# Four-way and eight-way interleaved moving operands in the out- and down-projection of a hybrid attention layer

## The chip, the cores and the metric

The kernel runs on one core of one Trainium2 chip. The metric is the device time of one execution in microseconds (us), as the median of a few runs. TensorE does the matmuls and its weight loads, VectorE (DVE), ScalarE (ACT) and GpSimd (POOL) do the elementwise work, and SyncE (SP) issues the transfers.

## The reference, cut to what matters

The layer works on 256 tokens of width 2048, all in float32:

```
h     = RMSNorm(x);  proj = h @ w_in            # 2048 x (6 * 1024 + 8)
o_f   = forgetting attention, 8 heads of 128    # group A
o_d   = differential attention, 8 heads of 128  # group B
x     = x + concat(o_f, o_d) @ w_out            # out-projection, 2048 x 2048
u     = RMSNorm(x) @ w_up                       # up-projection, 2048 x 11008
u     = causal conv of width 3 along the tokens
out   = x + (silu(gate) * val) @ w_down         # down-projection, 5504 x 2048
```

## The kernel before, in words

The reference is float32, and the matmuls are in a faster float32 form (`F32R`) that keeps fewer bits. So each operand is split into a rounded part (hi) and the rest (lo). ACT writes hi as a rounding copy (`split_hi`, line 534, for weights), DVE writes lo as the difference (`split_lo`, line 816). A product is the sum of hi x hi, hi x lo and lo x hi.

All weights stream in pieces of 128 x 1024 (128 x 768 for the input projection) through a ring of four slots: SP loads `raw`, ACT makes `w_hi`, DVE makes `w_lo`, and PE uses the piece and frees it (`piece_used`). PE works through the stages in this order: the input projection for one head after another, with the attention of the previous head laid between its pieces by hand; the out-projection (32 pieces, 256 weight blocks of 128 x 128); the up-projection (172 pieces); the down-projection (86 pieces, 688 weight blocks).

In the last three stages the weights are the stationary operand and the activations move. One weight block takes two matmuls (`mm3_features`, lines 277 to 281). The first (line 279) has the hi weights and moves 512 columns: hi and lo of one activation tile of 256 tokens. The second (line 280) has the lo weights and moves the 256 hi columns. The first writes a whole PSUM bank of 512 columns, the second adds into the upper half of that bank. So hi x hi stands in the lower half and the two mixed products in the upper half, and the result is the sum of both halves.

The columns do not move in the order in which they lie in SBUF. `weave` reads the tile alternately from two places that are 256 elements (1024 bytes) apart: element 0, element 256, element 1, element 257, and so on. `part` gives the layout of a tile that goes with it: with two ways a tile is [hi of tokens 0-127, lo of tokens 0-127, hi of 128-255, lo of 128-255], so that alternating reads give first all hi columns and then all lo columns, with tokens 0, 128, 1, 129, ... in this order. PSUM therefore holds the tokens of the out- and down-projection in alternating order, and `by_parity` reads them back with a step of two elements where the sum is taken (lines 1113 and 1115 for the out-projection, 1214 and 1220 for the down-projection); `by_half` walks the natural order in SBUF beside it. `mixed` holds the activation tiles of the out-projection (written at lines 592 and 934), `a_s` those of the down-projection (lines 771 and 1170), `xs` those of the up-projection (lines 737 and 1120), which are laid out so that PSUM comes out in natural order.

In the down-projection eight output tiles are summed at once, one for each bank: all 43 pieces of the first eight tiles, then all 43 of the second eight. The first piece of the second eight has to wait tile by tile until DVE has read the bank (`o_done`).

Before any weights land, PE runs 19 matmuls on a tile of ones, `warm_r`, in four shapes; the weights of each are columns 0 to 127 of the same tile:

```
for _ in range(WARM_UP + 2):                     # 10, line 375: 512 columns as they lie
...
for rhs in (weave(warm_r[:]), warm_r[:].rearrange("p (a b) -> p b a", a=4), weave(warm_r[:, 0:S])):
    for _ in range(3):                           # line 378: three of each
```

Of the kernel before, what the change touches and what calls it, by code (L numbers as in the profile page):

```python
# [9 lines left out]
ALU = mybir.AluOpType  # L10
ACT = mybir.ActivationFunctionType
AX_X = mybir.AxisListType.X

P = 128
S, D, F = 256, 2048, 5504
# [4 lines left out]
KT = D // P  # L20
# [7 lines left out]
RING = 4  # L28
# [9 lines left out]
DOWN0 = UP0 + UP_PIECES  # L38
ALL_PIECES = DOWN0 + DOWN_PIECES
OCTET = 8  # L40
SROW = P + S


# [19 lines left out]
def hybrid_layer_kernel(nc, xT_d, xtok_d, w0_d, win_d, wrest_d, const_d, row_d, vec_d, out_d):  # L63
    c_d = nc.dram_tensor("c_scratch", (H, S), F32, kind="Internal").ap()
    with ExitStack() as ctx:
# [8 lines left out]
        w_hi = sb("w_hi", RING * PW, F32R)  # L74
        w_lo = sb("w_lo", RING * PW, F32R)
        xT = sb("xT", KT * S)
# [12 lines left out]
        a_t = sb("a_t", S)  # L89
        xu = sb("xu", 2 * S)  # L90
        ms2 = y2_t[:, S:2 * S]

        with ExitStack() as att:
            def sa(name, cols, dt=F32, parts=P):
                return sb(name, cols, dt, parts, att)
            mixed = sa("mixed", KT * 2 * S, F32R)
# [37 lines left out]
        a_s = sb("a_s", FT * 2 * S, F32R)  # L134
# [25 lines left out]
        mixhi_done, mixlo_done = sem("mixhi_done"), sem("mixlo_done")  # L160
# [4 lines left out]
        xu_done, x1_done, x1hi_done, x1sq_done = sem("xu_done"), sem("x1_done"), sem("x1hi_done"), sem("x1sq_done")  # L165
# [3 lines left out]
        a_done, a_hi, a_lo = sem("a_done"), sem("a_hi"), sem("a_lo")  # L169
# [4 lines left out]
        def bank(b, lo=0, n=512):  # L174
            return ps[:, b * 512 + lo:b * 512 + lo + n]

        def f32(ap):
            return ap.bitcast(F32)

        def slot(t, s, n=PW, at=0):  # L180
            return t[:, s * PW + at:s * PW + at + n]

        def tile(t, i, n=S, width=S, at=0):

            return t[:, bass.ds(i * width + at, n)]

        def weave(ap):

            return ap.rearrange("p (k q) -> p q k", k=2)

        def part(t, h):

            return t.rearrange("p (k h j) -> p h k j", k=2, h=2)[:, h]

        def by_half(ap):
            return ap.rearrange("p (k j) -> p k j", k=2)

        def by_parity(ap):
            return ap.rearrange("p (j k) -> p k j", k=2)

        ident = const[:, C_ID:C_ID + P]
        block = ctx.enter_context(nc.Block())
# [61 lines left out]
        def _(pe):  # L264
# [9 lines left out]
                    last = pe.matmul(o, xl, wh, start=False, stop=(kt == KT - 1), skip_group_check=True)  # L274
                return last

            def mm3_features(b, s, t, acts, start, stop):

                pe.matmul(bank(b), slot(w_hi, s, P, t * P), weave(acts), start=start, stop=False, skip_group_check=True)  # L279
                return pe.matmul(bank(b, S, S), slot(w_lo, s, P, t * P), part(acts, 0).rearrange("p k j -> p j k"),  # L280
                                 start=False, stop=stop, skip_group_check=True)

            def transposes(f, p, kind):
# [92 lines left out]
            for rhs in (weave(warm_r[:]), warm_r[:].rearrange("p (a b) -> p b a", a=4), weave(warm_r[:, 0:S])):  # L376
                for _ in range(3):
                    pe.matmul(scratch[:, 0:rhs.shape[1] * rhs.shape[2]], warm_r[:, 0:P], rhs, start=True, stop=True,
                              skip_group_check=True)

            for g, (h, b) in enumerate(PAIR):
                pe.wait_ge(split_done, g + 1)
                for k2 in range(2):
                    if h == 0:
                        pe.wait_ge(xs_ready, 2 * b + k2 + 1)
                    last = mm3_tokens(h, QKV if h else QKV + H, 2 * b + k2, g % RING, k2)
# [42 lines left out]
            for b in range(8):  # L429
                pe.wait_ge(split_done, OUT0 + b + 1)  # L430

                for t in (0, 1, 4, 5, 2, 6, 3, 7) if b == 0 else range(8):
                    kt, n = 2 * b + t // 4, t % 4
                    if b == 0 and t == 0:
                        pe.wait_ge(evac_done, 4 * (HEADS - 1))
                    if b == 0 and t in (2, 3):
                        pe.wait_ge(evac_done, 4 * HEADS - 3 + t)
                    if kt >= KT - 2 and n == 0:
                        pe.wait_ge(mixlo_done, kt + 1)
                    mxt = mixed[:, kt * 2 * S:(kt + 1) * 2 * S]  # L440
                    last = mm3_features(n, b % RING, t, mxt, kt == 0, kt == KT - 1)
                last.then_inc(piece_used, 1)
                attention_steps(HEADS, 1, "fox", b, OUT_AT)

            def out_pair(i, first):

                for b in range(4):
                    pe.wait_ge(split_done, i * 4 + (OUT0 + 8 + b + 1))
                    if b % 2 == 0 and not first:
                        pe.wait_ge(x1_done, i * 2 + (3 + b // 2))  # L450
                    for t in range(8):
                        kt = 8 * (b % 2) + t
                        mxt = mixed[:, kt * 2 * S:(kt + 1) * 2 * S]
                        last = mm3_features(4 + b // 2, b, t, mxt, kt == 0, kt == KT - 1)
                    last.then_inc(piece_used, 1)

            out_pair(0, True)
# [26 lines left out]
            def down_piece(d, kt, s, edge=None):  # L484

                pe.wait_ge(split_done, d + (DOWN0 + 1))
                if edge == "start0":
                    pe.wait_ge(a_lo, FT - 2)
                    pe.wait_ge(r2_ready, 1)
                for n in range(OCTET):  # L490
                    if edge == "start0" and n == 6:
                        pe.wait_ge(g_sum, FT)
                        pe.wait_ge(v_sum, FT)
                    if edge == "start1":
                        pe.wait_ge(o_done, n + 1)
                    last = mm3_features(n, s, n, tile(a_s, kt, 2 * S, 2 * S),
                                        edge in ("start0", "start1"), False)
                last.then_inc(piece_used, 1)

            def last_two(d, s):  # L500

                pe.wait_ge(split_done, DOWN0 + d + 2)
                for n in range(OCTET):
                    for k in range(2):
                        kt = FT - 2 + k
                        a = a_s[:, kt * 2 * S:(kt + 1) * 2 * S]
                        last = mm3_features(n, s + k, n, a, False, k == 1)
                    if n < OCTET - 1:
                        last.then_inc(tile_summed, 1)
                last.then_inc(piece_used, 2)  # L510
# [17 lines left out]
        def _(act):  # L528
# [59 lines left out]
            def mix_hi(f, kind):  # L588

                act.wait_ge(pv_done if kind == "fox" else onorm_done, f)  # L590
                src = bank(B_O, 0, S) if kind == "fox" else on[:]
                act.activation(part(tile(mixed, f - 1, 2 * S, 2 * S), 0), by_half(src), ACT.Copy).then_inc(mixhi_done, 1)

            def square_o(f):
                act.wait_ge(pv_done, f)
# [59 lines left out]
            for b in range(4):  # L655
                if b == 2:
                    act.wait_ge(piece_used, PAIR_END0)
                    for m in range(M):
                        last = act.activation(z[:, m * H:(m + 1) * H], bank(m, QKV, H), ACT.Copy)
# [108 lines left out]
            def act_hi(i):  # L768

                act.wait_ge(a_done, i + 1)  # L770
                act.activation(part(tile(a_s, i, 2 * S, 2 * S), 0), by_half(a_t[:]), ACT.Copy).then_inc(a_hi, 1)

            def up_frame(i, first):
                for b in range(4):
# [38 lines left out]
        def _(dve):  # L813
# [116 lines left out]
            def mix_lo(f, kind):  # L930
                dve.wait_ge(mixhi_done, f)
                src = bank(B_O, 0, S) if kind == "fox" else on[:]
                mxt = tile(mixed, f - 1, 2 * S, 2 * S)
                dve.tensor_tensor(part(mxt, 1), by_half(src), part(f32(mxt), 0), ALU.subtract).then_inc(mixlo_done, 1)

            def forget_bias(f):

# [171 lines left out]

            def x1_tile(n, b, par):  # L1110

                u = by_half(xu[:, par * S:(par + 1) * S])
                dve.tensor_tensor(u, by_parity(bank(b, S, S)), by_half(tile(xT, n)), ALU.add).then_inc(xu_done, 1)
                dve.wait_ge(xu_done, n + 1)
                dve.tensor_tensor(by_half(tile(xT, n)), by_parity(bank(b, 0, S)), u, ALU.add).then_inc(x1_done, 1)  # L1115

            def x1_lo(n):
                dve.wait_ge(x1hi_done, n + 1)
# [48 lines left out]
            def act_lo(i):  # L1167
                dve.wait_ge(a_hi, i + 1)
                ast = tile(a_s, i, 2 * S, 2 * S)
                dve.tensor_tensor(part(ast, 1), by_half(a_t[:]), part(f32(ast), 0), ALU.subtract).then_inc(a_lo, 1)  # L1170

            def up_frame(i, first):

# [30 lines left out]
            def out_octet(o):  # L1204

                partial = [xu[:, 0:S], xu[:, S:2 * S], a_t[:], silu_t[:]]

                def add_second(n):
                    t = OCTET * o + n
                    if n < OCTET - 1:  # L1210
                        dve.wait_ge(tile_summed, (OCTET - 1) * o + n + 1)
                    else:
                        dve.wait_ge(piece_used, DOWN0 + FT * (o + 1))
                    dve.tensor_tensor(by_half(partial[n % 4]), by_parity(bank(n, S, S)), by_half(xT[:, t * S:(t + 1) * S]),
                                      ALU.add).then_inc(ou_done, 1)

                def add_first(n):
                    t = OCTET * o + n
                    dve.wait_ge(ou_done, t + 1)
                    dve.tensor_tensor(by_half(xT[:, t * S:(t + 1) * S]), by_parity(bank(n, 0, S)), by_half(partial[n % 4]),  # L1220
                                      ALU.add).then_inc(o_done, 1)

                add_second(0)
                for n in range(1, OCTET):
                    add_second(n)
                    add_first(n - 1)
                add_first(OCTET - 1)
# [138 lines left out]
```

## Time and profile before

| | |
|---|---|
| median of 3 runs | 1083.84 us (1083.58 to 1085.18) |
| the profiled execution | 1086.33 us |
| its span, first to last instruction | 1084.6 us |
| PE busy | 1063.9 us, 98% of the span |
| PE weight loads busy | 988.6 us, 91% |
| DVE / ACT / POOL busy | 774.7 / 626.1 / 132.0 us |
| read from HBM | 208.81 MB |

A matmul's busy time runs from its start to the modelled end of its drain, so successive matmuls overlap; the pace of PE is read from the starts of successive matmuls, not from the duration of one. PEclk is the clock granted to TensorE, as a share of full speed.

### The profile page before, as it was taken

To read this page: it belongs to the slowest core of one execution; us is meant where nothing else is said; L and a number is where in the kernel's file an instruction comes from. 1 tells how busy PE (TensorE), PEld (TensorE's weight loads), DVE (VectorE), ACT (ScalarE), POOL (GpSimd) and SP (SyncE) were. 2 spreads that over 40 slices of the span, in tenths; PEclk is the share of its full clock that TensorE was granted. 3 is DMA by queue.
4 is the path that set the end of the run, shared out by engine and by line. 5 is a ranking of instruction groups with operands and counts; after the bars stand their busy time and mean duration, and the time that the engine had idled before them with its cause. 6 is when DMAs were issued, how large, how long until landed. Compare 5 with 4: busy or idle time off the path is not lost.

```text
span 1084.6 us, 20254 instructions
## 1 busy us (share of the span) xinstructions
PE 1063.9 (98%) x6487; PEld 988.6 (91%) x6487; DVE 774.7 (71%) x1274; ACT 626.1 (58%) x1009; POOL 132.0 (12%) x170
## 2 busy tenths in 40 slices
PE   9889999999999999999999999999999999999998
PEld 8878988999998999999999999999999999999997
DVE  6677787776676877887887788787787744464444
ACT  6756665756565656666666666666666534334432
POOL 0222243000000212211111111111111100000000
PEclk9999999999999999999999999999999999999999
DMA  9654545465655765666666666666665666656664
GB/s 312 245 151 159 166 148 172 147 198 152 204 193 172 230 205 184 208 206 196 200 202 200 199 197 205 197 207 196 195 210 195 201 205 196 202 181 215 201 204 138
DMA packets 66762, 211.28 MB, mean 195 GB/s; under 512 B 9384, under 2 KB 11568, under 8 KB 66352
## 3 DMA queue, kind: packets, MB, share of 16 engines
q1 hardware_dynamic: 66736, 210.94, 61.1%
q8 instruction: 15, 0.25, 0.1%
q14 instruction: 11, 0.09, 0.0%
HBM read 208.81 MB, written 2.11 MB: 194 GB/s over the span
## 4 chain that ended last, share of the span: by engine, by line
PE 84%; DVE 7%; ACT 3%; POOL 2%; DMA 2%; issue 1%; SPq 0%; DVEq 0%; ACTq 0%; POOLq 0%
PE ps L279 45%; PE ps L280 23%; PE ps L272 4%; PE ps L274 4%; PE ps L273 4%; DVE w_lo L816 2%; DMA raw<-in_w 1%; ACT w_hi L534 1%; POOL qn L1251 1%; ACT s_sb L580 1%; DMA raw<-in_win 1%; DVE s_sb L884 1%; PE ps L289 1%; PE ps L298 1%; PE ps L318 0%
## 5 line engine op out<-in xcount | busy, mean ns | idle before, releaser
L816 DVE TENSOR_TENSOR w_lo<-raw,w_hi 128x1024 fp32r<-128x1024 f32 (+2 forms) x418 | 497.8, 1198 | 235.1 <-ACT w_hi L534 234.0
L534 ACT ACTIVATE w_hi<-raw 128x1024 fp32r<-128x1024 f32 (+2 forms) x418 | 414.0, 994 | 335.9 <-PE ps L280 272.0
L279 PE MATMUL ps<-xs,w_hi 128*128 128x512 f32 x1376 | 451.0, 382 | 0.0
L280 PE MATMUL ps<-xs,w_lo 128*128 128x256 f32 x1376 | 375.1, 273 | 0.0
L279 PEld LDWEIGHTS ps<-xs,w_hi 128*128 128x128 f32 x1376 | 260.1, 189 | 36.2
L280 PEld LDWEIGHTS ps<-xs,w_lo 128*128 128x128 f32 x1376 | 264.2, 192 | 0.0
L279 PE MATMUL ps<-a_s,w_hi 128*128 (+1 forms) x688 | 225.6, 382 | 0.1
L280 PE MATMUL ps<-a_s,w_lo 128*128 (+1 forms) x688 | 187.5, 273 | 0.0
L272 PE MATMUL ps<-w_hi,xs 128*128 128x384 f32 (+1 forms) x512 | 175.0, 342 | 2.3 <-DVE cT L1018 1.2
L273 PE MATMUL ps<-w_lo,xs 128*128 128x384 f32 (+1 forms) x512 | 167.6, 327 | 0.0
L274 PE MATMUL ps<-w_hi,xs 128*128 128x384 f32 (+1 forms) x512 | 167.6, 327 | 0.0
L279 PEld LDWEIGHTS ps<-a_s,w_hi 128*128 128x128 f32 x688 | 130.0, 189 | 18.6 <-DVE xT L1220 0.4
L280 PEld LDWEIGHTS ps<-a_s,w_lo 128*128 128x128 f32 x688 | 132.1, 192 | 0.0
L1296 POOL TENSOR_TENSOR u_t<-s_t,r2bc 128x256 f32<-128x256 f32 x86 | 71.6, 832 | 378.5 <-DVE s_t L1148 378.5
L272 PEld LDWEIGHTS ps<-w_hi,xs 128*128 128x128 f32 x512 | 97.4, 190 | 5.8 <-issue 2.3
L273 PEld LDWEIGHTS ps<-w_lo,xs 128*128 128x128 f32 x512 | 97.5, 190 | 0.3
L274 PEld LDWEIGHTS ps<-w_hi,xs 128*128 128x128 f32 x512 | 97.2, 190 | 0.0
L279 PE MATMUL ps<-mixed,w_hi 128*128 128x512 f32 x256 | 84.9, 384 | 0.5 <-DVE xT L1115 0.4
L280 PE MATMUL ps<-mixed,w_lo 128*128 128x256 f32 x256 | 69.8, 273 | 0.0
L757 ACT ACTIVATE y_t<-u_t,vec 128x256 f32<-128x256 f32 x86 | 51.5, 599 | 11.3 <-issue 6.1
L279 PEld LDWEIGHTS ps<-mixed,w_hi 128*128 128x128 f32 x256 | 48.4, 189 | 7.7 <-DVE xT L1115 0.7
L766 ACT ACTIVATE lo_t<-ps 128x256 f32<-128x256 f32 x86 | 32.5, 378 | 32.1 <-PE ps L280 32.1
(141 smaller groups left out, 705.3 us busy)
## 6 DMA issues: line engine op xcount, KB each, us to landing
raw<-in_wrest SPq DMA_DIRECT2D x290, 512.0 KB, 4.2
raw<-in_win SPq DMA_DIRECT2D x120, 384.0 KB, 3.7
raw<-in_w SPq DMA_DIRECT2D x8, 392.0 KB, 5.5
xT<-in_xT SPq DMA_DIRECT2D x8, 256.0 KB, 5.7
xtok<-in_xtok SPq DMA_DIRECT2D x2, 1024.0 KB, 8.2
out<-xT SPq DMA_DIRECT2D x16, 128.0 KB, 2.2
cbc<-c_scratch SPq DMA_DIRECT2D x1, 1024.0 KB, 6.8
const<-in_const SPq DMA_DIRECT2D x1, 512.0 KB, 9.3
```

The source lines that it names most:

```text
L272: pe.matmul(o, xh, wh, start=(kt == 0), stop=False, skip_group_check=True)
L273: pe.matmul(o, xh, wl, start=False, stop=False, skip_group_check=True)
L274: last = pe.matmul(o, xl, wh, start=False, stop=(kt == KT - 1), skip_group_check=True)
L279: pe.matmul(bank(b), slot(w_hi, s, P, t * P), weave(acts), start=start, stop=False, skip_group_check=True)
L280: return pe.matmul(bank(b, S, S), slot(w_lo, s, P, t * P), part(acts, 0).rearrange("p k j -> p j k"), start=False, stop=stop, skip_group_c ...
L289: last = pe.transpose(bank(B_T, i * P, P), qn[:, c:c + HD], ident)
L298: last = pe.matmul(bank(B_S + c, P, S), qkT[rows, P:S], qkT[rows, S:2 * S], start=True, stop=True, skip_group_check=True)
L534: act.activation(slot(w_hi, s, w), slot(raw, s, w), ACT.Copy).then_inc(hi_ready, 1)
L757: act.activation(y2_t[:, y2:y2 + S], u_t[:, u + 2:u + 2 + S], ACT.Identity, scale=tile(vec, i, 1, 8, V_CW + off + 2), bias=tile(vec, i, 1, ...
L766: act.activation(lo_t[:, lo:lo + S], bank(6 + (not gate), S, S), ACT.Copy).then_inc(g_lo if gate else v_lo, 1)
L816: dve.tensor_tensor(slot(w_lo, s, w), slot(raw, s, w), f32(slot(w_hi, s, w)), ALU.subtract).then_inc(split_done, 1)
L1296: pool.tensor_tensor(u_t[:, u:u + S], s_t[:, off:off + S], r2bc[:], ALU.mult).then_inc(g_u if gate else v_u, 1)
```

## The change: more places to read from

The four layout helpers get a parameter for the number of ways, 2 by default. The out-projection uses 4, the down-projection 8. With 4 ways a tile of 512 elements is four stretches of [64 hi, 64 lo], and the moving operand is read from four places 128 elements (512 bytes) apart in turn; with 8 ways it is eight stretches of [32 hi, 32 lo], read from eight places 64 elements (256 bytes) apart. The writers of `mixed` and `a_s` use the same layouts, and the sums are read from PSUM with a step of 4 or 8 elements. The input projection, the up-projection, the warm-up matmuls, the number and size of all instructions, the waits and the transfers stay as they are.

```diff
+OUT_WAYS, DOWN_WAYS = 4, 8
...
-        def weave(ap):
-            return ap.rearrange("p (k q) -> p q k", k=2)
-        def part(t, h):
-            return t.rearrange("p (k h j) -> p h k j", k=2, h=2)[:, h]
+        def weave(ap, k=2):
+            return ap.rearrange("p (k q) -> p q k", k=k)
+        def part(t, h, k=2):
+            return t.rearrange("p (k h j) -> p h k j", k=k, h=2)[:, h]
...
-            def mm3_features(b, s, t, acts, start, stop):
-                pe.matmul(bank(b), slot(w_hi, s, P, t * P), weave(acts), start=start, stop=False, skip_group_check=True)
-                return pe.matmul(bank(b, S, S), slot(w_lo, s, P, t * P), part(acts, 0).rearrange("p k j -> p j k"),
+            def mm3_features(b, s, t, acts, start, stop, k=2):
+                pe.matmul(bank(b), slot(w_hi, s, P, t * P), weave(acts, k), start=start, stop=False, skip_group_check=True)
+                return pe.matmul(bank(b, S, S), slot(w_lo, s, P, t * P), part(acts, 0, k).rearrange("p k j -> p j k"),
                                  start=False, stop=stop, skip_group_check=True)
...
-                u = by_half(xu[:, par * S:(par + 1) * S])
-                dve.tensor_tensor(u, by_parity(bank(b, S, S)), by_half(tile(xT, n)), ALU.add).then_inc(xu_done, 1)
+                u = by_half(xu[:, par * S:(par + 1) * S], OUT_WAYS)
+                dve.tensor_tensor(u, by_parity(bank(b, S, S), OUT_WAYS), by_half(tile(xT, n), OUT_WAYS), ALU.add).then_inc(xu_done, 1)
...
-                    dve.tensor_tensor(by_half(xT[:, t * S:(t + 1) * S]), by_parity(bank(n, 0, S)), by_half(partial[n % 4]),
+                    dve.tensor_tensor(by_half(xT[:, t * S:(t + 1) * S], DOWN_WAYS), by_parity(bank(n, 0, S), DOWN_WAYS),
+                                      by_half(partial[n % 4], DOWN_WAYS),
                                       ALU.add).then_inc(o_done, 1)
```

## Rows read from the trace of the kernel before

**Rows 1.** The page: busy time by engine, granted clock.

```profile
PE 1063.9 (98%) x6487; PEld 988.6 (91%) x6487; DVE 774.7 (71%) x1274; ACT 626.1 (58%) x1009; POOL 132.0 (12%) x170
...
PEclk9999999999999999999999999999999999999999
```

**Rows 2.** Stages out (two rows), up, down (two): busy us of each engine, PEclk, DMA.

```profile
318.63:351.54 32.91, 32.47 (x199) 29.66 (x200) 22.51 (x45) 17.67 (x29) 2.67 (x4) 1.00 0.50 160
351.54:403.90 52.36, 52.36 (x319) 48.23 (x320) 42.04 (x53) 31.65 (x43) 10.14 (x11) 1.00 0.69 217
403.90:855.20 451.30, 451.30 (x2757) 415.02 (x2757) 360.46 (x518) 285.22 (x431) 71.58 (x86) 1.00 0.63 200
855.20:970.15 114.95, 114.88 (x703) 105.23 (x701) 59.61 (x65) 48.01 (x48) 0.73 (x1) 1.00 0.61 197
970.15:1081.10 110.95, 110.95 (x676) 101.86 (x676) 54.55 (x55) 41.34 (x39) 0.00 (x0) 1.00 0.58 189
```

**Rows 3.** The page, costliest groups: the matmuls of the two changed stages, with counts.

```profile
L279 PE MATMUL ps<-a_s,w_hi 128*128 (+1 forms) x688 | 225.6, 382 | 0.1
L280 PE MATMUL ps<-a_s,w_lo 128*128 (+1 forms) x688 | 187.5, 273 | 0.0
...
L279 PE MATMUL ps<-mixed,w_hi 128*128 128x512 f32 x256 | 84.9, 384 | 0.5 <-DVE xT L1115 0.4
L280 PE MATMUL ps<-mixed,w_lo 128*128 128x256 f32 x256 | 69.8, 273 | 0.0
```

**Rows 4.** Timeline of PE in the down-projection: start us, us, engine, line, operation.

```profile
999.73 0.38 PE L279 MATMUL ps<-a_s,w_hi 128*128 x1
999.95 0.27 PE L280 MATMUL ps<-a_s,w_lo 128*128 x1
...
1002.68 0.38 PE L279 MATMUL ps<-a_s,w_hi 128*128 x1
```

**Rows 5.** Timeline of PE, warm-up: three 2-way, three 4-way, then 2-way of 256.

```profile
5.90 0.63 PE L378 MATMUL ps<-warm_r 128*128 128x512 f32 x1
6.32 0.63 PE L378 MATMUL ps<-warm_r 128*128 128x512 f32 x1
6.74 0.45 PE L378 MATMUL ps<-warm_r 128*128 128x512 f32 x1
7.03 0.44 PE L378 MATMUL ps<-warm_r 128*128 128x512 f32 x1
7.31 0.45 PE L378 MATMUL ps<-warm_r 128*128 128x512 f32 x1
7.59 0.45 PE L378 MATMUL ps<-warm_r 128*128 128x512 f32 x1
7.87 0.39 PE L378 MATMUL ps<-warm_r 128*128 128x256 f32 x2
7.98 0.39 PE L378 MATMUL ps<-warm_r 128*128 128x256 f32 x2
```

**Rows 6.** Timeline of the weight loads (PEld) in the same stretch.

```profile
6.75 0.26 PEld L378 LDWEIGHTS ps<-warm_r 128*128 128x128 f32 x1
7.03 0.19 PEld L378 LDWEIGHTS ps<-warm_r 128*128 128x128 f32 x1
```

**Rows 7.** Timeline of PE, input projection, 2-way reads of 384 columns (11 starts apart).

```profile
12.27 0.33 PE L272 MATMUL ps<-w_hi,xs 128*128 128x384 f32 x1
...
14.06 0.33 PE L274 MATMUL ps<-w_hi,xs 128*128 128x384 f32 x1
```

**Rows 8.** Groups by line and shape: DVE adds that read PSUM unstrided, with step two.

```profile
L1148 DVE TENSOR_TENSOR s_t<-ps,lo_t 128x256 f32<-128x256 f32 x86 | 35.9, 418 | 0.0
...
L1115 DVE TENSOR_TENSOR xT<-ps,xu 128x256 f32 x12 | 5.1, 424 | 0.4
```

**Rows 9.** Chain of waits where the second octet starts: start us, us, what.

```profile
965.12 0.67 DVE xu L1214 x2
...
970.15 0.48 PE ps L279
```

More of the change, by code:

```diff
@@ L185, in tile, with by_half, by_parity @@
             return t[:, bass.ds(i * width + at, n)]
-        def weave(ap):
-            return ap.rearrange("p (k q) -> p q k", k=2)
-        def part(t, h):
-            return t.rearrange("p (k h j) -> p h k j", k=2, h=2)[:, h]
[L195 to L199, printed above, removed]
+        def weave(ap, k=2):
+            return ap.rearrange("p (k q) -> p q k", k=k)
+        def part(t, h, k=2):
+            return t.rearrange("p (k h j) -> p h k j", k=k, h=2)[:, h]
+        def by_half(ap, k=2):
+            return ap.rearrange("p (k j) -> p k j", k=k)
+        def by_parity(ap, k=2):
+            return ap.rearrange("p (j k) -> p k j", k=k)
         ident = const[:, C_ID:C_ID + P]
@@ L440, in _ @@
                     mxt = mixed[:, kt * 2 * S:(kt + 1) * 2 * S]
-                    last = mm3_features(n, b % RING, t, mxt, kt == 0, kt == KT - 1)
+                    last = mm3_features(n, b % RING, t, mxt, kt == 0, kt == KT - 1, OUT_WAYS)
                 last.then_inc(piece_used, 1)
@@ L453, in out_pair @@
                         mxt = mixed[:, kt * 2 * S:(kt + 1) * 2 * S]
-                        last = mm3_features(4 + b // 2, b, t, mxt, kt == 0, kt == KT - 1)
+                        last = mm3_features(4 + b // 2, b, t, mxt, kt == 0, kt == KT - 1, OUT_WAYS)
                     last.then_inc(piece_used, 1)
@@ L496, in down_piece @@
                     last = mm3_features(n, s, n, tile(a_s, kt, 2 * S, 2 * S),
-                                        edge in ("start0", "start1"), False)
+                                        edge in ("start0", "start1"), False, DOWN_WAYS)
                 last.then_inc(piece_used, 1)
@@ L506, in last_two @@
                         a = a_s[:, kt * 2 * S:(kt + 1) * 2 * S]
-                        last = mm3_features(n, s + k, n, a, False, k == 1)
+                        last = mm3_features(n, s + k, n, a, False, k == 1, DOWN_WAYS)
                     if n < OCTET - 1:
@@ L591, in mix_hi @@
                 src = bank(B_O, 0, S) if kind == "fox" else on[:]
-                act.activation(part(tile(mixed, f - 1, 2 * S, 2 * S), 0), by_half(src), ACT.Copy).then_inc(mixhi_done, 1)
+                act.activation(part(tile(mixed, f - 1, 2 * S, 2 * S), 0, OUT_WAYS), by_half(src, OUT_WAYS), ACT.Copy).then_inc(mixhi_done, 1)
             def square_o(f):
@@ L770, in act_hi @@
                 act.wait_ge(a_done, i + 1)
-                act.activation(part(tile(a_s, i, 2 * S, 2 * S), 0), by_half(a_t[:]), ACT.Copy).then_inc(a_hi, 1)
+                act.activation(part(tile(a_s, i, 2 * S, 2 * S), 0, DOWN_WAYS), by_half(a_t[:], DOWN_WAYS), ACT.Copy).then_inc(a_hi, 1)
             def up_frame(i, first):
@@ L933, in mix_lo @@
                 mxt = tile(mixed, f - 1, 2 * S, 2 * S)
-                dve.tensor_tensor(part(mxt, 1), by_half(src), part(f32(mxt), 0), ALU.subtract).then_inc(mixlo_done, 1)
+                dve.tensor_tensor(part(mxt, 1, OUT_WAYS), by_half(src, OUT_WAYS), part(f32(mxt), 0, OUT_WAYS), ALU.subtract).then_inc(mixlo_done, 1)
             def forget_bias(f):
@@ L1110, in x1_tile @@
             def x1_tile(n, b, par):
-                u = by_half(xu[:, par * S:(par + 1) * S])
-                dve.tensor_tensor(u, by_parity(bank(b, S, S)), by_half(tile(xT, n)), ALU.add).then_inc(xu_done, 1)
+                u = by_half(xu[:, par * S:(par + 1) * S], OUT_WAYS)
+                dve.tensor_tensor(u, by_parity(bank(b, S, S), OUT_WAYS), by_half(tile(xT, n), OUT_WAYS), ALU.add).then_inc(xu_done, 1)
                 dve.wait_ge(xu_done, n + 1)
-                dve.tensor_tensor(by_half(tile(xT, n)), by_parity(bank(b, 0, S)), u, ALU.add).then_inc(x1_done, 1)
+                dve.tensor_tensor(by_half(tile(xT, n), OUT_WAYS), by_parity(bank(b, 0, S), OUT_WAYS), u, ALU.add).then_inc(x1_done, 1)
             def x1_lo(n):
@@ L1169, in act_lo @@
                 ast = tile(a_s, i, 2 * S, 2 * S)
-                dve.tensor_tensor(part(ast, 1), by_half(a_t[:]), part(f32(ast), 0), ALU.subtract).then_inc(a_lo, 1)
+                dve.tensor_tensor(part(ast, 1, DOWN_WAYS), by_half(a_t[:], DOWN_WAYS), part(f32(ast), 0, DOWN_WAYS), ALU.subtract).then_inc(a_lo, 1)
             def up_frame(i, first):
@@ L1213, in add_second @@
                         dve.wait_ge(piece_used, DOWN0 + FT * (o + 1))
-                    dve.tensor_tensor(by_half(partial[n % 4]), by_parity(bank(n, S, S)), by_half(xT[:, t * S:(t + 1) * S]),
+                    dve.tensor_tensor(by_half(partial[n % 4], DOWN_WAYS), by_parity(bank(n, S, S), DOWN_WAYS),
+                                      by_half(xT[:, t * S:(t + 1) * S], DOWN_WAYS),
                                       ALU.add).then_inc(ou_done, 1)
```

## The prediction

> **What bounds the kernel now.** I read the page first, then the stages, then the starts of single matmuls. The page shows PE busy for 98% of the span, its clock at full in every slice, and DVE and ACT well below [rows 1]. A table by stage says the same of both stages that change: PE is busy for all but 0.5 us of the five rows, while DVE is at 45 to 55 us of 110 in the down-projection and at 42 of 52 in the main part of the out-projection [rows 2]. So the time of these stages is the number of matmuls times the pace at which PE starts them, and each nanosecond on one of them counts in full. There are 256 weight blocks in the out-projection and 688 in the down-projection, each one matmul of 512 columns and one of 256 [rows 3].
>
> The duration in rows 3 is no pace (successive matmuls overlap). The starts give it: in the down-projection nine blocks take from 999.73 to 1002.68, 2.95 us, so 0.328 us each; the 512 columns take 0.22 of it (999.73 to 999.95), by columns 0.2185, and the 256 columns 0.109 [rows 4]. At 2.4 GHz, one column a cycle, 768 columns would take 0.320 us. A two-way read is therefore at 2.4% of what the array can take, and that is all that a better read order could win.
>
> **Does the trace show a four-way read? It does.** The warm-up has three matmuls of each of three shapes on line 378, and the second three read 512 columns from four places, 128 elements apart: exactly the operand that the out-projection gets. The starts stand in rows 5. The first two (two-way) start 0.42 and 0.43 us apart, 1.2 GHz for 512 columns, as TensorE was still at its lower level. The third starts at 6.74 and the next at 7.03; its weight load takes 0.26 us, the next one 0.19 [rows 5, 6], and 0.19 is what the ones behind it take too, so the clock rose within this matmul and everything from 7.03 on runs at 2.4 GHz. From there the four-way ones start at 7.03, 7.31, 7.59, and the next shape at 7.87: 0.28 us each, three times. The two-way 256 columns behind them start at 7.87 and 7.98: 0.11, as in rows 4. So at the full clock a 512-column read costs 0.2185 two-way and 0.280 four-way, a factor of 1.28, or +0.0615 us. DMA traffic doesn't explain it, since the 256-column ones stand in the same burst of loads, and neither do the weights, which come from columns 0 to 127 of that tile in both shapes.
>
> **The out-projection.** First matmul: 256 x 0.0615 = 15.7 us. The second one reads 256 columns from four places; the trace has no such shape. Bounds: 0, and the same factor, 0.109 x 0.28 = 0.031 each. I take the factor, since a cost that hangs on the read order is paid per column: 256 x 0.031 = 7.9 us. Together +23.6 us (15.7 with the lower bound for the second).
>
> **The down-projection.** No row shows eight ways. The lower end is the pace that the array allows, 0.320 a block (-0.008); then two-way pace (0). The upper end is the slowest pace of a 512-column matmul in the trace, 0.42 (the two slow ones of rows 5, nearly half speed), a factor of 1.92, or +0.302 a block. Between them lie the four-way factor, 0.420 a block, and one more step of the same factor, 1.28 x 1.28 = 1.64, 0.538 a block. I take the four-way factor: whatever is missed when the read returns to a place only after four columns is missed too when it returns after eight, and the four-way row is the nearest. 688 x (0.0615 + 0.031) = +63.6 us.
>
> The Trainium skill has a rule on this, in "SBUF — State Buffer", section "Door 1: The DMA port swizzle": SBUF is read by 16-byte lines, a line needs at least two successive hits for full speed, and each access that goes to another line pays. Taken by the letter, two-way, four-way and eight-way reads are all the same, for in each of them every access goes to another line than the one before; the sum would then be 0. The trace speaks against the letter: two-way reads are within 2.4% of one column a cycle, and four-way reads are not.
>
> **The rest.** The writers of `mixed` and `a_s` and the `by_half` operands walk shorter contiguous runs; their instructions, 16 and 86 of 0.42 us or less, lie on engines with room [rows 2], so they are taken at 0. The 64 adds that read PSUM with a step of 4 or 8: a step of two costs 424 ns against 418 without one [rows 8], so I take +0. Their upper bound is a doubling, +0.42 us; cover exists except at the switch between the octets, where PE waits until the last of 16 chained adds has freed its bank (965.12 to 970.15 in the chain, [rows 9]), in the tail with 16 more, and in the first eight of the out-projection: 40 x 0.21 = 8 us if half of each doubling shows. With PE slower, ACT and DVE have more slack in splitting weights, and no new wait arises: SP, ACT and DVE all wait for `piece_used`, which comes later, not earlier. The 0.5 us in which PE was idle in these stages [rows 2] is left as it is.
>
> **Sum.** 23.6 + 63.6 = +87.2 us. On the profiled execution's 1086.3 us (span 1084.6 and 1.7 around it) this is 1173.5. That execution is 2.5 us above the median of the runs shown, 1083.8, so I say 1171 us.
>
> **The rivals.**
>
> A2. Only the 512-column matmuls lose (something that needs a long read): 944 x 0.0615 = 58.1, so 1142. For it: the two-way rows show 0.109 for 256 and nothing of four. Against: a pattern cost should not know the length.
>
> A3. Eight ways cost more than four: with one more step of the factor, (0.538 - 0.328) x 688 = 144.5 and 23.6, so 1252; at half speed 0.302 x 688 = 207.8 and 23.6, so 1315. For it: from two to four places the pace fell at once. Against: nothing else.
>
> A4. Eight places 256 bytes apart avoid what four places 512 bytes apart meet, and the down-projection keeps its pace: 1084 + 24 = 1108.
>
> B. No difference. The four-way warm-ups are slow for a reason of their own (the tile serves weights and moving columns at once, 19 matmuls into one bank), or the rule of the skill holds by the letter. Then 1084. Against: the 256-column ones share the tile, the bank and the weights.
>
> C. Faster, the other side. The 512-column two-way read is the only one with an excess: 384 columns two-way take (14.06 - 12.27) / 11 = 0.1627 us [rows 7], 0.424 ns a column, which for a block of 768 makes 0.3255 against 0.328. If more places remove that excess, each of 944 blocks gains 0.0025 us: 2.4 us, so 1081.4. It holds from the point at which the fetch of 512 columns at 1024 bytes apart is what costs, and four or eight places are not worse than two; the end of its scale is 0.320 a block, 944 x 0.008 = 7.5 us, 1076. Only the warm-up rows speak against it.
>
> **How the numbers follow.** The forecast (all reads by the four-way factor) gets 0.51, A2 0.09, A3 0.11 for 1252 and 0.05 for 1315, A4 0.08, B 0.07, C 0.09. Slower by over 0.2% (2.2 us, about what a measurement of this kernel can tell from no change) is everything but B and C: 0.84. Same is 0.07, faster 0.09. The range from 1100 to 1275 holds the forecast, A2, A4 and the first part of A3, 0.79; left out are B and C below and half speed above.
>
> **What would show it right or wrong.** In the changed kernel the starts of successive 512-column matmuls in the out-projection should be 0.28 us apart from the next 256-column one, and those 0.14 from the following; the stage from 318.6 to 403.9 grows by 24 us. The up-projection, at 0.328 a block, must not change, nor PEclk. In the down-projection the block pace is the open number: 0.42 by the forecast, 0.54 or 0.63 by A3, 0.328 by A4. The mean of the adds on lines 1214 and 1220, 416 to 418 ns now, tells what a step of eight costs. Starts 0.218 apart in the out-projection would make the whole forecast wrong, and the warm-up rows a bad witness.

## The result and the profile after

| | before | changed |
|---|---|---|
| median of 4 runs | 1083.82 us | 1388.03 us (1386.81 to 1388.56) |
| the profiled execution | 1086.33 us | 1388.56 us |
| its span | 1084.6 us | 1386.7 us |

The changed kernel is slower by 304.2 us, a ratio of 1.2802 (95% interval 1.278 to 1.2824). The forecast said 1171 us, range 1100 to 1275: the sign and the place were right, the growth was forecast too small by a factor of 3.5 (87 against 304 us).

The page's first lines, of the changed kernel. Against [rows 1], PE has 304 us more and is as full as before; the clock is full in every slice; DVE and ACT do the same work in a longer span.

```profile
PE 1367.6 (99%) x6487; PEld 1077.0 (78%) x6487; DVE 777.8 (56%) x1274; ACT 624.6 (45%) x1009; POOL 130.0 (9%) x170
...
PEclk9999999999999999999999999999999999999999
```

The table by stage of the changed kernel (out-projection, up-projection, down-projection; columns as in [rows 2]). The up-projection, untouched, takes 451.2 us, as before (451.3). The out-projection takes 110.8 where its two rows and the 1.5 us ahead of them made 86.8, the down-projection 504.6 where its two rows made 225.9: 24 and 279 us longer, with 87 GB/s of transfers where there were 189 to 197: everything else waits for PE.

```profile
316.60:427.40 110.80, 110.80 (x527) 87.22 (x526) 67.01 (x97) 50.05 (x75) 11.37 (x15) 1.00 0.47 156
427.40:878.60 451.20, 451.20 (x2757) 414.84 (x2756) 360.28 (x517) 284.58 (x431) 71.36 (x86) 1.00 0.63 200
878.60:1383.20 504.60, 504.60 (x1378) 287.34 (x1376) 115.53 (x119) 89.78 (x87) 0.74 (x1) 1.00 0.26 87
```

The timeline of PE in both stages of the changed kernel (lines 280 and 281 are the former 279 and 280), to be read against [rows 4]: the starts are what counts.

```profile
359.60 0.45 PE L280 MATMUL ps<-mixed,w_hi 128*128 128x512 f32 x1
359.88 0.31 PE L281 MATMUL ps<-mixed,w_lo 128*128 128x256 f32 x1
...
362.16 0.45 PE L280 MATMUL ps<-mixed,w_hi 128*128 128x512 f32 x1
```

```profile
1299.55 0.67 PE L280 MATMUL ps<-a_s,w_hi 128*128 x1
1300.04 0.42 PE L281 MATMUL ps<-a_s,w_lo 128*128 x1
...
1303.22 0.67 PE L280 MATMUL ps<-a_s,w_hi 128*128 x1
```

Four places: six blocks in 2.56 us, 0.427 a block, 0.28 of it for 512 columns. Eight places: five blocks in 3.67 us, 0.734 a block, 0.49 for 512 columns and 0.24 for 256. The two paces account for the whole result: 256 x 0.099 + 688 x 0.406 = 25 + 279 = 304 us.

The groups of the changed kernel's adds from PSUM, with a step of 8 and of 4, against [rows 8]: 423 and 424 ns where an unstrided one takes 418.

```profile
L1116 DVE TENSOR_TENSOR xT<-ps,xu 128x256 f32 x12 | 5.1, 424 | 0.4
...
L1215 DVE TENSOR_TENSOR xu<-ps,xT 128x256 f32<-128x256 f32 x8 | 3.4, 423 | 14.7 <-PE ps L281 14.7
```

### The profile page after: what moved, and what is told of

It is laid out like the page before. It is cut to its first block, busy times and chain, and to the rows that moved or that the text cites. A ratio compares the mean times of both kernels' runs of the same rounds, so it can differ in the third digit from the quotient of the medians.

```text
span 1386.7 us, 20254 instructions
## 1 busy us (share of the span) xinstructions
PE 1367.6 (99%) x6487; PEld 1077.0 (78%) x6487; DVE 777.8 (56%) x1274; ACT 624.6 (45%) x1009; POOL 130.0 (9%) x170
## 4 chain that ended last, share of the span: by engine, by line
PE 88%; DVE 4%; ACT 2%; DMA 2%; POOL 2%; issue 1%; SPq 0%; DVEq 0%; POOLq 0%
PE ps L280 51%; PE ps L281 26%; PE ps L273 3%; PE ps L275 3%; PE ps L274 3%; DVE w_lo L817 1%; DMA raw<-in_w 1%; ACT w_hi L535 1%; POOL qn L1254 1%; ACT s_sb L581 1%; DVE s_sb L885 1%; DMA raw<-in_win 1%; PE ps L290 0%; PE ps L299 0%; DMA raw<-in_wrest 0%
## 5 line engine op out<-in xcount | busy, mean ns | idle before, releaser
L280 PE MATMUL ps<-a_s,w_hi 128*128 (+1 forms) x688 | 461.0, 670 | 0.0
L280 PEld LDWEIGHTS ps<-a_s,w_hi 128*128 128x128 f32 x688 | 143.1, 208 | 192.4 <-issue 192.1
L281 PE MATMUL ps<-a_s,w_lo 128*128 (+1 forms) x688 | 291.0, 423 | 0.0
L281 PEld LDWEIGHTS ps<-a_s,w_lo 128*128 128x128 f32 x688 | 144.5, 210 | 24.3
L280 PE MATMUL ps<-mixed,w_hi 128*128 128x512 f32 x256 | 109.6, 449 | 0.0
L281 PE MATMUL ps<-mixed,w_lo 128*128 128x256 f32 x256 | 78.8, 308 | 0.0
L1160 DVE SCALAR_TENSOR_TENSOR y_t<-u_t,vec,y_t 128x256 f32<-128x256 f32 x86 | 41.8, 486 | 12.9 <-DVE y_t L1157 12.8
```

What stands on the lines that cost most here:

```text
L280: pe.matmul(bank(b), slot(w_hi, s, P, t * P), weave(acts, k), start=start, stop=False, skip_group_check=True)
L1160: dve.scalar_tensor_tensor(out=y, in0=u_t[:, u:u + S], scalar=tile(vec, i, 1, 8, V_CW + c), in1=y1, op0=ALU.mult, op1=ALU.add).then_inc(g_ ...
```

## The experiments

The runs of the kernel before that stand beside them have medians of 1085.32 us (e1 to e4), 1085.31 (e5, e6) and 1084.72 (e7, e8); ratios are to these.

### One part at a time: e2 and e3

```diff
-OUT_WAYS, DOWN_WAYS = 4, 8
+OUT_WAYS, DOWN_WAYS = 4, 2        # e2
+OUT_WAYS, DOWN_WAYS = 2, 4        # e3
```

> Four places in the out-projection only. With the paces read in the changed kernel (0.283 + 0.143 a block against 0.218 + 0.109), both theories: 256 x 0.099 = 25 us over the kernel before, 1109 us.

> Two places in the out-projection, four in the down-projection. If the four-way pace is a property of the read order and not of the stage: 688 x 0.099 = +68 us, 1152 us. If the down-projection has a cost of its own (its operands, its eight banks), a four-way block there costs more than 0.426 us.

Measured: e2 1109.82 us, ratio 1.0222 (1.0179 to 1.0266); e3 1152.11 us, ratio 1.0612 (1.0571 to 1.0653). Where either kernel reads four places, its pace is that of the changed kernel's out-projection: in e3's down-projection, the starts of the timeline are 0.28 and 0.14 or 0.15 apart.

```profile
1099.94 0.45 PE L280 MATMUL ps<-a_s,w_hi 128*128 x1
1100.22 0.31 PE L281 MATMUL ps<-a_s,w_lo 128*128 x1
1100.36 0.45 PE L280 MATMUL ps<-a_s,w_hi 128*128 x1
```

So the pace belongs to the read order, not to the stage. Four places were priced rightly; eight are a price of their own.

### One place: e4

```diff
+OUT_WAYS, DOWN_WAYS = 1, 1
```

> Both projections read their columns as they lie, one place after another (all hi, then all lo), and sums are read from PSUM without a step. Theory W: one place is the end of the series, 0.325 a block or a little less, 944 x 0.0025 = 2 us faster, 1081 us. A theory in which the alternation itself is what keeps the pace (successive columns of one line wait for each other): slower than two places, up to 0.427 per 512 columns, 1370 us.

Measured 1101.1 us, ratio 1.0142 (1.0103 to 1.0182), neither of the two. In its down-projection two blocks take from 999.62 to 1000.31, 0.345 each, 0.0175 more than with two places; x 944 = 16.5 us.

```profile
999.62 0.39 PE L280 MATMUL ps<-a_s,w_hi 128*128 x1
999.85 0.28 PE L281 MATMUL ps<-a_s,w_lo 128*128 x1
...
1000.31 0.39 PE L280 MATMUL ps<-a_s,w_hi 128*128 x1
```

Two is a real optimum between one and four: the alternation buys some 10 ns on each matmul of these stages, and on one of 512 columns four places cost 65 ns and eight 270. "The fewer places, the better" (theory W) falls with it.

### Which orders are slow: e1

Groups of eight matmuls after the warm-up, each group on a line of its own, from one tile of ones:

```diff
+            def ways(k, apart):      # k places in turn, that many elements apart
+                return probe[:, 0:k * apart].rearrange("p (k q) -> p q k", k=k)[:, 0:{3: 128, 6: 64}.get(k, 512 // k), :]
+            def near(k, apart):      # the same inside blocks of k * apart elements
+                return probe[:, 0:512].rearrange("p (b k q) -> p b q k", k=k, q=apart)
+            def step(n):             # one stream, every n-th element
+                return probe[:, 0:512 * n].rearrange("p (q n) -> p q n", n=n)[:, :, 0]
+            def runs(k, j):          # j elements in a row from each of k places
+                return probe[:, 0:512].rearrange("p (k a j) -> p a k j", k=k, j=j)
```

> The kernel before with 37 groups of 8 further warm-up matmuls ahead of its work (about 110 us), each of 512 columns (384 for six places) from one stretch of ones, each group with another read order on a line of its own. Pace is (duration of the group less one duration) / 7. Theory W (a few 16-byte lines are kept open, and the number of places decides): 2 places 0.218 us at any distance; 4 places 0.283 at 16, 64, 256, 528, 768 or 4096 bytes apart; 8 places 0.49 at any distance; 16 places at least 0.49; one place 0.216; steps of 4 and 8 elements in a single stream slow (0.43 or more), since each column is on a new line; step of 2 between. Theory D (places whose distance is a multiple of 256 bytes meet the same part of the memory): 4 places 132, 144 or 130 elements apart, and 8 places 68, 66 or 80 apart, drop to 0.218, and near places too; 128, 192 and 1024 apart stay slow. Theory R (each return of the access pattern to its first place costs): two places worst, which the stages of this case already contradict.

The timeline of PE in this kernel: start of a group, its length, and the line. The pace is the distance to the next group's start, divided by 8. The orders are, from the top: L404 one place, L406 two places 16 bytes apart, L408 the order 0, 2, 1, 3 within one line of 16 bytes, L410 two places 256 bytes apart; L418 six places 512 bytes apart (384 columns); L420 four places 512 bytes apart, L422 256 bytes apart; L438 eight places 256 bytes apart, L440 16 bytes apart; L458 and L460 one stream with a step of 2 and 4; L464, L466 and L468 two places by twos, two by fours, four by twos; L470 and L474 four and eight places by fours.

```profile
17.76 2.02 PE L404 MATMUL ps<-mixed,warm_r 128*128 128x512 f32 x8
19.62 1.89 PE L406 MATMUL ps<-mixed,warm_r 128*128 128x512 f32 x8
21.34 2.03 PE L408 MATMUL ps<-mixed,warm_r 128*128 128x512 f32 x8
23.21 1.89 PE L410 MATMUL ps<-mixed,warm_r 128*128 128x512 f32 x8
24.93 1.89 PE L412 MATMUL ps<-mixed,warm_r 128*128 128x512 f32 x8
...
30.11 2.04 PE L418 MATMUL ps<-mixed,warm_r 128*128 128x384 f32 x8
31.98 2.41 PE L420 MATMUL ps<-mixed,warm_r 128*128 128x512 f32 x8
34.22 2.44 PE L422 MATMUL ps<-mixed,warm_r 128*128 128x512 f32 x8
36.49 2.32 PE L424 MATMUL ps<-mixed,warm_r 128*128 128x512 f32 x8
...
51.88 4.14 PE L438 MATMUL ps<-mixed,warm_r 128*128 128x512 f32 x8
55.84 4.02 PE L440 MATMUL ps<-mixed,warm_r 128*128 128x512 f32 x8
59.68 3.69 PE L442 MATMUL ps<-mixed,warm_r 128*128 128x512 f32 x8
...
88.67 3.80 PE L458 MATMUL ps<-mixed,warm_r 128*128 128x512 f32 x8
92.29 3.87 PE L460 MATMUL ps<-mixed,warm_r 128*128 128x512 f32 x8
95.99 3.63 PE L462 MATMUL ps<-mixed,warm_r 128*128 128x512 f32 x8
99.44 2.79 PE L464 MATMUL ps<-mixed,warm_r 128*128 128x512 f32 x8
102.06 2.18 PE L466 MATMUL ps<-mixed,warm_r 128*128 128x512 f32 x8
104.08 3.78 PE L468 MATMUL ps<-mixed,warm_r 128*128 128x512 f32 x8
107.68 2.34 PE L470 MATMUL ps<-mixed,warm_r 128*128 128x512 f32 x8
109.86 4.12 PE L472 MATMUL ps<-mixed,warm_r 128*128 128x512 f32 x8
113.79 2.40 PE L474 MATMUL ps<-mixed,warm_r 128*128 128x512 f32 x8
116.03 1.90 PE L476 MATMUL ps<-mixed,warm_r 128*128 128x512 f32 x8
```

In us for 512 columns: one place 0.233; two places 0.215, at 16 bytes as at 256, and the same at 1024, 1028, 1040 and 4096 bytes; four places 0.280 and 0.284; eight 0.495 and 0.480. Over all distances that were tried, 16 bytes to 4096 for four places, four take 0.269 to 0.284 and eight 0.439 to 0.495 (theory D falls: places moved off multiples of 256 bytes take 2% to 5% less with four and 3% to 11% less with eight, not half). Sixteen places are not slower than eight: 0.434 and 0.461. DVE, ACT and the transfers do nothing during these groups (0 GB/s), so other traffic to SBUF has no part in these paces.

Three rows fit neither W nor D. A single stream with a step of two elements takes 0.4525, as much as one with a step of four (0.4625), though it uses each 16-byte line twice in a row. The order 0, 2, 1, 3 within a line is as fast as 0, 1, 2, 3 (0.234). And two places read by twos are slow, 0.3275, against 0.215 for the same places read one by one. All three make sense if even and odd columns are fetched apart. With step 2, the even columns are elements 0, 4, 8: a new line each time. By twos, the even columns are 0, 256, 2, 258, so that one side goes back and forth between two lines; one by one, each side stays in its own place.

The idea orders these rows, but it doesn't size all of them. Places read by fours give each side two hits in a row on a line, as one place does, and take 0.2525 (two places), 0.2725 (four) and 0.280 (eight) against 0.2325. Six places, three lines a side, take 0.234 for 384 columns, which is 0.312 for 512: nearer to four places than to eight. Why is open.

### Even and odd columns: e5

```diff
+            def sparse(k, apart, n):   # k places in turn, every n-th element in each
+                return probe[:, 0:k * apart].rearrange("p (k q n) -> p q k n", k=k, n=n)[:, 0:512 // k, :, 0]
+            def shared(order):         # "p q h k": A, B, A+2, B+2;  "p q k h": A, A+2, B, B+2
+                a = probe[:, 0:1024].rearrange("p (k q h n) -> p k q h n", k=2, h=2, n=2)[:, :, :, :, 0]
+                return a.rearrange("p k q h -> " + order)
```

> The kernel before with 19 groups of 8 further warm-up matmuls ahead of its work. Theory E (even and odd columns are fetched separately, side by side, each side at half the array's pace; a side keeps up while its own successive columns fall into one 16-byte line, and pays for each line it goes to): the order A, B, A+2, B+2 (two places, each side stays in one line for two columns) about 0.23 us for 512 columns; the same elements in the order A, A+2, B, B+2, where each side changes lines with every column, 0.43 or more; two places with a step of 2 elements in each 0.23, though a single stream with step 2 took 0.45; two places with a step of 4, and one stream with a step of 3, 0.43 or more; four places with step 2 each 0.33. Theory L (one set of line buffers for the whole stream, the number of lines touched decides): the two orders of A, A+2, B, B+2 cost the same; two places with step 2 cost what the single stream with step 2 did, 0.45. Lengths: four places at 256 columns 0.143, eight places at 256 and 128 columns 0.243 and 0.12, as in the stages. The 512 and 256 pair: 0.216 + 0.109 if the 0.218 of the stages comes from their operands, 0.218 + 0.109 if from the pair.

The timeline of PE, read as before. L403 is A, B, A+2, B+2; L405 is A, A+2, B, B+2; L407 two places with step 2; L409 two with step 4; L411 four with step 2; L413 one stream with step 3; L415 and L417 four and eight places at 256 columns.

```profile
18.12 2.02 PE L403 MATMUL ps<-mixed,warm_r 128*128 128x512 f32 x8
19.98 4.06 PE L405 MATMUL ps<-mixed,warm_r 128*128 128x512 f32 x8
23.86 2.04 PE L407 MATMUL ps<-mixed,warm_r 128*128 128x512 f32 x8
25.74 3.79 PE L409 MATMUL ps<-mixed,warm_r 128*128 128x512 f32 x8
29.35 2.80 PE L411 MATMUL ps<-mixed,warm_r 128*128 128x512 f32 x8
31.98 3.77 PE L413 MATMUL ps<-mixed,warm_r 128*128 128x512 f32 x8
35.57 1.32 PE L415 MATMUL ps<-mixed,warm_r 128*128 128x256 f32 x8
36.73 2.36 PE L417 MATMUL ps<-mixed,warm_r 128*128 128x256 f32 x8
38.90 1.28 PE L419 MATMUL ps<-mixed,warm_r 128*128 128x128 f32 x8
```

The same elements in two orders: 0.2325 and 0.485. Two places with step 2 take 0.235, where one stream with that step took 0.4525. With step 4 0.451, four places with step 2 0.329, step 3 0.449. All six came within 3% of what theory E gave, or fell on its side of a bound, and the first two contradict theory L. A miss: eight places at 256 columns take 0.271 here and 0.243 in the stage, at 128 columns 0.136 where 0.12 was expected; why is open.

### In the kernel: e6, e7 and e8

e6 keeps every layout and step of the changed kernel and changes the order in which PE walks the tile; the output is written where it stood before. e7 does it with four places at a time (`g = 4`). The matmul with the lo weights is changed alike.

```diff
-                pe.matmul(bank(b), slot(w_hi, s, P, t * P), weave(acts, k), start=start, stop=False, skip_group_check=True)
...
+                g = min(k, 4)                    # e7; e6 has 2 in the place of g
+                m = k // g
+                two = acts.rearrange("p (m k q) -> p m q k", m=m, k=g)
...
+                pe.matmul(bank(b).rearrange("p (q m k) -> p m q k", m=m, k=g), slot(w_hi, s, P, t * P), two,
+                          start=start, stop=False, skip_group_check=True)
```

> The changed kernel with its 4-way and 8-way layouts in SBUF and PSUM and its sums with steps of 4 and 8 all kept, but PE walks each tile two places at a time: places 0 and 1 alternately to their end, then 2 and 3, and so on, and writes each pair of columns to where it stood. If the order of the reads alone is the cause (theories E and L): 1084 us, as the kernel before, or a few us more if writing pairs of columns with a gap costs something. If the layouts, the steps in the sums or the short stretches are part of it, between 1084 and 1388; the adds alone could make up to 8 us.

> The changed kernel with all its layouts and steps kept; PE walks four places at a time (in the out-projection that is all four; in the eight-way tiles places 0 to 3, then 4 to 7). If the cost is that of the number of places in turn: 0.283 + 0.143 a block in both stages, 944 x 0.099 = 93 us over the kernel before, 1177 us. This is also what the forecast gave the changed kernel (1171) by taking eight places at the four-way price. If the eight-way layout itself costs, it stays near 1388.

e6 takes 1084.83 us, ratio 1.0001 (0.9991 to 1.0011). The whole 304 us are gone although the tiles lie in eight stretches and the sums are read with a step of 8. In its down-projection (lines 283 and 285 are the former 279 and 280) a block takes 0.33 again:

```profile
1000.24 0.38 PE L283 MATMUL ps<-a_s,w_hi 128*128 x1
1000.46 0.27 PE L285 MATMUL ps<-a_s,w_lo 128*128 x1
1000.57 0.38 PE L283 MATMUL ps<-a_s,w_hi 128*128 x1
```

e7 takes 1176.67 us, ratio 1.0839 (1.0801 to 1.0877): the eight-way layout, read four at a time, costs what four places cost. It is also within 6 us of the forecast, which had charged eight places at that price.

e8 starts from the other side: two places, 1024 bytes apart, as in the kernel before, but two columns in a row from each.

```diff
+                    runs = acts.rearrange("p (k a j) -> p a k j", k=2, j=2)
+                    hi = acts.rearrange("p (k h a j) -> p h a k j", k=2, h=2, j=2)[:, 0]
```

> The layouts of the kernel before (two places, 1024 bytes apart) in both projections, but two columns in a row from each: 0, 1, 256, 257, 2, 3, 258, 259. Sums are read from PSUM in that order. Places, lines touched and distances are those of the kernel before. Theory E (even and odd columns fetched apart): the even side now goes 0, 256, 2, 258, so each side goes back and forth between two lines; 0.327 for 512 columns as the same order took in the first set of shapes, half of it for 256, 0.49 a block: 944 x 0.163 = +154 us, 1238 us. Theory L (the number of lines or places of the whole stream): as before, 1084 us, or better, since there are half as many jumps.

Measured 1250.89 us, ratio 1.1523 (1.1485 to 1.1561). The timeline of its down-projection has three blocks in 1.51 us, 0.503 each, where 0.49 was expected and 0.328 is the pace before.

```profile
1149.98 0.50 PE L289 MATMUL ps<-a_s,w_hi 128*128 x1
1150.31 0.34 PE L291 MATMUL ps<-a_s,w_lo 128*128 x1
...
1151.49 0.51 PE L289 MATMUL ps<-a_s,w_hi 128*128 x1
```

The number of places, their distance, the lines touched and the layout are those of the fast kernel; only which columns are neighbours has changed (and with it the order in which DVE reads the sums, at 415 to 425 ns an add), and it costs 166 us. A theory that counts places or lines of the whole stream, as W and L do, doesn't survive this.

No kernel here beats the one before: two places one by one are the fastest order of all that were tried.

## Why the prediction was wrong

- **What bounds the kernel.** Right. PE's pace in the two stages makes the whole difference, and nothing hidden came up: no wait on DVE, ACT or the transfers grew into the path. One row was misread without harm: DVE's busy time in the two rows of the down-projection [rows 2] is 59.6 and 54.6 us, and 45 to 55 is not what they say.
- **The witness.** Right. The three four-way warm-up matmuls, 0.28 us each, were the pace of the four-way stage, 0.28 as well. Reading the clock's rise from paces and weight loads was the step that made them usable: the granted clock reads 1.00 in all of the warm-up, also where the matmuls start 0.42 apart. In e2 the clock rose earlier, and there the three two-way ones of the same line start 0.215 apart and the four-way ones 0.28.
- **The out-projection.** +23.6 us forecast, +25 measured. The 256-column matmul pays per column as assumed (0.143 against 0.109; 0.031 extra was forecast, 0.034 came). Rival A2 is dead.
- **The down-projection.** This is the step that failed, and with it the forecast: "whatever is missed when the read returns to a place only after four columns is missed too when it returns after eight". It took 0.0925 us extra a block; 0.406 came, 279 us instead of 63.6. In the series two, four, eight places the paces are 0.218, 0.28 and 0.49. By theory E, what is missed is not the place but the line: with four places each side alternates between two lines, and pays a part; with eight it goes round four, and the pace (0.44 to 0.495 by the distance) is about that of a stream with a step of 3 or 4 (0.45 to 0.46), which goes to a new line with every column or nearly so. Rival A3 named the direction, but its one more step of 1.28 gave 0.538 a block against 0.734.
- **The upper bound.** It was 0.42 for 512 columns, from two-way matmuls on the slower clock level. That row shows how slow a two-way read is at the lower clock, and nothing in it bounds a slower read order at the full clock; 0.49 lies above it. The 1315 us worked out from it as the far end is still 73 us below the result, and the range stopped at 1275.
- **The rule on 16-byte lines.** In the letter of the Trainium skill's page ("SBUF — State Buffer", "Door 1: The DMA port swizzle"), two hits on a line give full speed. The trace of before spoke against it for two places. The runs mend it in one point: hits have to be counted for even and odd columns apart. Two in a row then keep 0.233 us (one place, or two places with a step of 2), and 0.2525 to 0.280 where the places are read by fours. One at a time costs 0.45 to 0.49 where a side goes to a new line with every column or round four lines, and less where it alternates between two (0.28 for four places, 0.3275 for two by twos) or goes round three (0.312 for six places). Four in a row, which of the orders tried only two places one by one give, keep 0.215.
- **The rest.** Strided sums: +0 forecast, 423 and 424 ns against 418; e6 has them all and runs at 1084.83.

That the order of the reads is the cause is shown by e6 and e8. That the fetch is split by even and odd columns is inferred from orders, not seen; e5 and e8 were forecast from it, and the rivals that were written down beside it fell. A fetch that takes two successive columns together, and pays where a pair needs other lines than the pair before it, would sort all these orders in the same way; no run here tells the two apart. Why eight places take between 0.439 and 0.495 by their distance is open.

## What to carry to other kernels

Take the order in which a float32 moving operand is read as a cost of its own (all runs here are in the `F32R` form): successive even columns should come from neighbouring elements, and so should successive odd ones, which two interleaved halves do and four or eight interleaved parts do not. If a layout needs more parts, walk them two at a time and let the output's access pattern put the columns in place, which cost nothing here. And when a row gives one step of a series, the next step has no bound from it: a price that doubles must be allowed for, and a row that is slow for one reason bounds nothing that is slow for another.

## What the hardware showed unexpectedly

Reading contiguous float32 columns is slower than reading two places in turn: 0.233 against 0.215 us for 512 columns, and 16 us in the kernel (e4).

Below 256 columns the length no longer sets the pace of matmuls that each load 128 columns of weights: with 256, 192 and 128 columns from two places they start 0.112, 0.108 and 0.109 us apart in e5 (the groups at 41.31, 42.21 and 43.07; the last one ends with the start at 43.94), and with 128 contiguous columns 0.105.

```profile
41.31 1.05 PE L423 MATMUL ps<-mixed,warm_r 128*128 128x256 f32 x8
42.21 1.03 PE L425 MATMUL ps<-mixed,warm_r 128*128 128x192 f32 x8
43.07 1.03 PE L427 MATMUL ps<-mixed,warm_r 128*128 128x128 f32 x8
43.94 1.16 PE L429 MATMUL ps<-mixed,warm_r 128*128 128x256 f32 x8
```

The excess of rival C may come from there. In the same run a pair of 512 and 256 columns is followed by the next after 0.327 us (six pairs from 46.16 to 48.12), and a pair of 512 and 384 columns after 0.378 (six from 48.83 to 51.10).

The second is 5 ns over one column a cycle at 2.4 GHz (0.373), the first 7 ns (0.320). So the 2 ns too many of a block go with the 256 columns and not with the read of 512. That 256 columns are a little too short to cover the load of the next weights would explain it, but is not shown. No read order tried here won them back.
